# Mixing of the second block: four differential maps a step, a running bank for the suffix sums, paired value products, a new order; two weight differences on VectorE

## What is computed

```python
# per layer l = 0, 1 of the second block
f = swiglu(rmsnorm(x, ffn1_pre_g[l]), ffn1_w_gate[l], ffn1_w_up[l], ffn1_w_down[l])
x = x + FFN_RESIDUAL_WEIGHT * rmsnorm(f, ffn1_post_g[l])
m = token_mixing(rmsnorm(x, mix_pre_g[l]), w_in[l], rel_bias[l], ..., w_out[l], lambda_init)
x = x + rmsnorm(m, mix_post_g[l])
f = swiglu(rmsnorm(x, ffn2_pre_g[l]), ...)

def diff_attention(q, k, v, lam, subln_g, lambda_init):      # 4 heads, two maps of 32 features each
    ...
        sc = jnp.einsum('bqhmd,bkhmd->bhmqk', q[:, q0:kend], k[:, :kend]).astype(jnp.float32) * scale
        sc = sc + alibi[None, :, None]
        sc = jnp.where(allowed[None, None, None], sc, NEG_INF)
        p = jax.nn.softmax(sc, axis=-1)
        w = p[:, :, 0] - lam * p[:, :, 1]
        outs.append(jnp.einsum('bhqk,bkhd->bqhd', w.astype(v.dtype), v[:, :kend]))
    ...
def stick_breaking_attention(q, k, v):                       # 6 heads of 64
    ...
        z = jnp.einsum('bqhd,bkhd->bhqk', q[:, q0:kend], k[:, :kend]).astype(jnp.float32) * scale
        log_beta = jax.nn.log_sigmoid(z)
        log_one_minus = jnp.where(strict, jax.nn.log_sigmoid(-z), 0.0)
        suffix = lax.cumsum(log_one_minus, axis=3, reverse=True) - log_one_minus
        a = jnp.where(strict, jnp.exp(log_beta + suffix), 0.0)
        outs.append(jnp.einsum('bhqk,bkhd->bqhd', a.astype(v.dtype), v[:, :kend]))
```

## Time and profile before

| | |
|---|---|
| median of 3 runs | 2588.81 us (2588.8 to 2589.32) |
| the profiled execution | 2589.32 us, its span 2587.5 us |
| TensorE busy | 2560.7 us, 99% of the span |
| VectorE, ScalarE, GpSimd busy | 1637.7, 1169.8, 423.3 us |
| TensorE's granted clock | 1.000 in the mean |
| mixing of layer 0 and of layer 1 | 982 to 1246 us and 1969 to 2233 us |
| HBM | 97 GB/s over the span |

### The profile page before, as it was taken

How to read it: one execution, slowest core, us unless ns; L and a number is a source line. 1 busy time by engine, 2 the same in 40 slices (tenths; PEclk the granted TensorE clock), 3 DMA queues, 4 the chain that set the end, 5 groups by cost and what they waited for, 6 DMA issues and landing times.

```text
span 2587.5 us, 42242 instructions
## 1 busy us (share of the span) xinstructions
PE 2560.7 (99%) x17332; PEld 2222.2 (86%) x17332; DVE 1637.7 (63%) x2667; ACT 1169.8 (45%) x2019; POOL 423.3 (16%) x416
## 2 busy tenths in 40 slices
PE   9999999999999999999999999999999999999998
PEld 7788887678999888867899988999888876899987
DVE  3425653667999353456699735899444356699833
ACT  4123333643655234465455533555334456355522
POOL 0230010001332011111143200233001020133200
PEclk9999999999999999999999999999999999999999
DMA  8722140012333232211233332332323212223321
GB/s 323 290 93 93 38 123 33 34 58 82 99 106 107 98 117 67 66 50 66 82 115 100 113 114 66 115 115 98 114 82 104 64 50 83 66 90 115 115 96 67
DMA packets 183854, 252.73 MB, mean 98 GB/s; under 512 B 13040, under 2 KB 158448, under 8 KB 179184
## 3 DMA queue, kind: packets, MB, share of 16 engines
q1 hardware_dynamic: 183664, 250.04, 29.0%
HBM read 247.92 MB, written 2.10 MB: 97 GB/s over the span
## 4 chain that ended last, share of the span: by engine, by line
PE 92%; DVE 3%; ACT 2%; issue 1%; DMA 1%; POOL 1%; SPq 0%; POOLq 0%; ACTq 0%; DVEq 0%
PE psum L816 89%; PE psum L1384 1%; DMA mod_w<-in_l_ab_w_mod 1%; PE psum L1268 1%; PE psum L884 1%; DVE stats_first L2206 0%; DVE work L2199 0%; ACT w_hi L1558 0%; DVE X L2202 0%; ACT work L1606 0%; POOL stats_first L2925 0%; PE psum L860 0%; DVE h_lo L2138 0%; DVE wide L2236 0%; POOL stats L2980 0%
## 5 line engine op out<-in xcount | busy, mean ns | idle before, releaser
L816 PE MATMUL psum<-h_hi,w_hi 128*128 128x256 f32 (+1 forms) x1520 | 498.2, 328 | 0.4 <-DVE w_lo L2105 0.3
L816 PE MATMUL psum<-h_lo,w_hi 128*128 128x256 f32 (+1 forms) x1520 | 490.9, 323 | 0.0
L816 PE MATMUL psum<-h_hi,w_lo 128*128 128x256 f32 (+1 forms) x1520 | 490.8, 323 | 0.0
L2105 DVE TENSOR_TENSOR w_lo<-raw,w_hi 128x2048 fp32r<-128x2048 f32 (+1 forms) x99 | 223.4, 2260 | 295.1 <-ACT w_hi L1558 294.6
L816 PEld LDWEIGHTS psum<-h_hi,w_hi 128*128 128x128 f32 x1520 | 290.0, 191 | 32.6 <-issue 9.7
L816 PEld LDWEIGHTS psum<-h_hi,w_lo 128*128 128x128 f32 x1520 | 289.6, 191 | 22.6
L816 PEld LDWEIGHTS psum<-h_lo,w_hi 128*128 128x128 f32 x1520 | 289.9, 191 | 20.0 <-issue 0.5
L1558 ACT ACTIVATE w_hi<-raw 128x2048 fp32r<-128x2048 f32 (+1 forms) x100 | 188.5, 1888 | 259.5 <-PE psum L816 249.5
L816 PE MATMUL psum<-w_hi,ff_hi 128*128 128x512 f32 x576 | 225.2, 391 | 1.2 <-DVE ff_lo L2722 1.2
L816 PE MATMUL psum<-w_lo,ff_hi 128*128 128x512 f32 x576 | 224.4, 390 | 0.0
L816 PE MATMUL psum<-w_hi,ff_lo 128*128 128x512 f32 x576 | 224.4, 390 | 0.0
(11 more groups left out here) (364 smaller groups left out, 5444.4 us busy)
## 6 DMA issues: line engine op xcount, KB each, us to landing
raw<-in_ffn_w_gate SPq DMA_DIRECT2D x44, 1024.0 KB, 5.2
raw<-in_ffn_w_up SPq DMA_DIRECT2D x44, 1024.0 KB, 5.2
raw<-in_ffn_w_down SPq DMA_DIRECT2D x44, 1024.0 KB, 4.7
raw<-in_w_in SPq DMA_DIRECT2D x36, 512.0 KB, 5.0
raw<-in_l_ab_w_in SPq DMA_DIRECT2D x10, 1024.0 KB, 9.3
mod_w<-in_l_ab_w_mod SPq DMA_DIRECT2D x8, 1024.0 KB, 17.9
raw<-in_w_out SPq DMA_DIRECT2D x8, 1024.0 KB, 4.8
raw<-in_cd_w_in SPq DMA_DIRECT2D x7, 1024.0 KB, 5.3
```

The costliest lines, as they stand in the source:

```text
L816: return pe.matmul(o, lhsT, rhs, start=start, stop=stop, skip_group_check=True)
L2105: dve.tensor_tensor(lo[:, 0:nk * n], raw[c % 2][:, 0:nk * n], hi[:, 0:nk * n].bitcast(F32), ALU.subtract).then_inc(*w_lo_made.mark(key))
```

## The change

- *Scores:* a step `diff_quad` multiplies the two maps of two heads, four products on four row groups, into four banks. The soft ring gets four banks, the stick ring keeps two.
- *Suffix sums:* a head's four stages share one bank and go from the last stage to the first. Each stage after the first waits until VectorE has subtracted the one before, adds the product of `strict` with that stage's softplus (triangle plus strict mask is all ones), and then the product of `tri` with its own. VectorE subtracts in the same order, and the bank comes free at the end.
- *Value products:* those of two heads follow each other directly and write to two halves of 128 columns of one bank (bands and differential heads); VectorE or ScalarE reads the first when both are done.
- *Order:* all four strings are new.
- *Feed-forward:* S3 and S4 move from GpSimd to VectorE, after the split of A22.

```diff
@@ mix_streams
-    streams["a"] = [step for i in range(0, len(bands), 2) for step in [("band_pair", *streams["a"][i][1:]), *streams["a"][i:i + 2]]]
+    for letter, both in (("a", "band_pair"), ("c", "band_value_pair"), ("d", "diff_quad"), ("g", "diff_value_pair")):
+        single = streams[letter]
+        streams[letter] = [step for i in range(0, len(single), 2) for step in [(both, *single[i][1:]), *single[i:i + 2]]]
...
-                           [("stick_sums", h, kt) for kt in range(NT)] + [("stick_exp", h)] + [("stick_value_pair", h)] * (letter == "s") +
+                           [("stick_sums", h, kt) for kt in reversed(range(NT))] + [("stick_exp", h)] + [("stick_value_pair", h)] * (letter == "s") +
@@ MIX_ENGINES, MIX_LETTERS (TensorE's string of before, then of after; the others are rewritten in the same way)
...
-    "pe": ("vppspspsaapbpbppppappbbppppcpcappppppppppcbcppcppttbppssbpdtpptppdfppadpssppsppcpppbpspspsfbpccpppabppppcppdpbafbdpppppc"
-           "ssgttgttpffgdpcsspdpppcsdfspspspbbppgappppfdggfdppdfpfdgpgpppfcdggppfdgcstbfdbggastfdccttssfabbsccabbgnfgccbbpcpaogcppnp"
-           "pppppnbobppppppccooprpppnpppppppprppppr"),
+    "pe": ("ppppaasppbpsbpsapppbpcpppbppppppppppppppppbscaptbpspsptsdpptcpbpppbpftpfppdscpppspsaapsppbppbppppppsgcpbfppsppbaptstdp"
+           "pfstppgcbftpfpspdpbpasppsgcspppppfpdpfpppfgsfpdppptbsbactsbgbtcfsnftdgsafppobabpfpgcppdnppbbpopcappfppbbppofncgppnpprp"
+           "pppprovpppppppr"),
@@ tensor_program, mixing
-                proj, soft, stick = Ring([0, 1]), Ring([2, 3, 4]), Ring([5, 6, 7])
+                proj, soft, stick = Ring([0, 1]), Ring([2, 3, 4, 5]), Ring([6, 7])
...
+                    at = b * BANK + 64 * (h % 2)
...
-                    elif kind == "diff_scores":
+                    elif kind == "diff_quad":
                         _, i, h, t = step
                         width = (t + 1) * P
...
+                        banks = [claim(soft.take(), ("bs", s, i + n // 2, n % 2)) for n in range(4)]
+                        if t == 0:
+                            pe.wait_ge(*mix_kept[s, 1408 + P * (h // 2)])
+                        for n, b in enumerate(banks):
+                            p0 = 32 * n
+                            done(mm(bank(b, width), q_b[p0:p0 + 32, h // 2, t * P:(t + 1) * P], k_b[p0:p0 + 32, h // 2, 0:width], True, True),
+                                 ("bs", s, i + n // 2, n % 2))
...
-                    elif kind == "diff_values":
+                    elif kind == "diff_value_pair":
...
+                        bank_of["bv", s, i + 1] = b
...
+                        for odd in range(2):
+                            pe.wait_ge(*probs_turned["b", s, i + odd])
+                            done(attend(v_b, h + odd, t, b, turned["b"][(i + odd) % 2]), ("bv", s, i + odd))
...
-                        b = claim(stick.take(), ("csum", s, h, kt))
-                        if kt == 0:
+                        if kt == NT - 1:
+                            claim(stick.take(), ("csum", s, h))
                             pe.wait_ge(*stick_cut[s, h])
                             pe.wait_ge(*stick_landed[layer])
-                        m = mm(bank(b, L - kt * P), tri[:, :], soft_[:, STARTS[kt]:STARTS[kt] + L - kt * P], True, kt == 3)
-                        for k2 in range(kt + 1, NT):
-                            m = mm(bank(b, L - k2 * P, (k2 - kt) * P), ones[:, :], soft_[:, STARTS[k2]:STARTS[k2] + L - k2 * P], False, k2 == 3)
+                        else:
+                            pe.wait_ge(*stick_dve["sums", s, h, kt + 1])
+                            mm(full(("csum", s, h), L - (kt + 1) * P, (kt + 1) * P), strict[:, 0, :], soft_[:, STARTS[kt + 1]:STARTS[kt + 1] + L - (kt + 1) * P],
+                               False, False)
+                        m = mm(full(("csum", s, h), L - kt * P, kt * P), tri[:, :], soft_[:, STARTS[kt]:STARTS[kt] + L - kt * P], kt == NT - 1, kt == 0)
                         done(m, ("csum", s, h, kt))
@@ vector_program, ffn
+                def last_mixed(key):
+
+                    s2, s3, s4 = (fast_weights(key, name)[2] for name in ("S2", "S3", "S4"))
+                    dve.tensor_tensor(s3, fast_block(key, 0, 0), fast_block(key, 0, 1), ALU.subtract).then_inc(*fast_mixed.mark((key, "S3")))
+                    dve.wait_ge(*fast_first[key, "S2"])
+                    dve.tensor_tensor(s4, fast_block(key, 1, 0), s2, ALU.subtract).then_inc(*fast_mixed.mark((key, "S4")))
...
                         lo_blocks(following, "A1")
                         lo_blocks(following, "A22")
+                        last_mixed(following)
@@ gpsimd_program
-                    if s[0] == "ffn":
-                        for q, key in enumerate(fast_keys(s[1], layer)):
...
-                            pool.tensor_tensor(mixed_["S3"], fast_block(key, 0, 0), fast_block(key, 0, 1), ALU.subtract).then_inc(*fast_mixed.mark((key, "S3")))
-                            pool.wait_ge(*fast_first[key, "S2"])
-                            pool.tensor_tensor(mixed_["S4"], fast_block(key, 1, 0), mixed_["S2"], ALU.subtract).then_inc(*fast_mixed.mark((key, "S4")))
```

More of the change, by code:

```diff
@@ L245 @@
 BAND_ITEM = {(step[2], step[3]): step[1] for step in MIX_ORDER["dve"] if step[0] == "band_scores"}
-DIFF_ITEM = {(step[2], step[3]): step[1] for step in MIX_ORDER["pe"] if step[0] == "diff_scores"}
+DIFF_ITEM = {(step[2], step[3]): step[1] for step in MIX_ORDER["dve"] if step[0] == "diff_scores"}
 def build(nc, A, out):
@@ L1433, in mixing @@
                         turn_probs(("at", s, i), band_slot(i), t)
-                    elif kind == "band_values":
+                    elif kind == "band_value_pair":
                         _, i, h, t = step
                         b = claim(soft.take(), ("av", s, i))
+                        bank_of["av", s, i + 1] = b
                         if h in (0, 4):
                             pe.wait_ge(*mix_kept[s, "v", int(h == 4), t])
-                        pe.wait_ge(*probs_turned["a", s, i])
-                        done(attend(v_a, h, t, b, turned["a"][i % 2]), ("av", s, i))
-                    elif kind == "diff_scores":
+                        for odd in range(2):
+                            pe.wait_ge(*probs_turned["a", s, i + odd])
+                            done(attend(v_a, h + odd, t, b, turned["a"][(i + odd) % 2]), ("av", s, i + odd))
+                    elif kind == "diff_quad":
                         _, i, h, t = step
                         width = (t + 1) * P
[L1444 to L1449, removed]
+                        banks = [claim(soft.take(), ("bs", s, i + n // 2, n % 2)) for n in range(4)]
[5 more added lines that the diff above has]
+                                 ("bs", s, i + n // 2, n % 2))
                     elif kind == "diff_turn":
@@ L1453, in mixing @@
                         turn_probs(("bt", s, i), map0[i % 2], t)
-                    elif kind == "diff_values":
+                    elif kind == "diff_value_pair":
                         _, i, h, t = step
                         b = claim(soft.take(), ("bv", s, i))
+                        bank_of["bv", s, i + 1] = b
                         if h == 0:
                             pe.wait_ge(*mix_kept[s, "v", 3, t])
-                        pe.wait_ge(*probs_turned["b", s, i])
-                        done(attend(v_b, h, t, b, turned["b"][i % 2]), ("bv", s, i))
+                        for odd in range(2):
+                            pe.wait_ge(*probs_turned["b", s, i + odd])
+                            done(attend(v_b, h + odd, t, b, turned["b"][(i + odd) % 2]), ("bv", s, i + odd))
                     elif kind == "stick_part":
@@ L2037, in mixing @@
                         event = ("bv", s, i)
-                        copy(o_tok[:, t, 384 + h * 64:384 + (h + 1) * 64], event, full(event, 64), attn_kept, (s, i), scale=stat("diff", i, 6, 7))
+                        act.wait_ge(*psum_full["bv", s, i | 1])
+                        copy(o_tok[:, t, 384 + h * 64:384 + (h + 1) * 64], event, full(event, 64, 64 * (h % 2)), attn_kept, (s, i), scale=stat("diff", i, 6, 7))
+                        freed["bv", s, i - h % 2] = attn_kept[s, i]
                     elif kind == "stick_scores":
@@ L2056, in mixing @@
                         z = stick_ring[h % 2][1]
-                        act.wait_ge(*stick_dve["sums", s, h, 3])
+                        act.wait_ge(*stick_dve["sums", s, h, 0])
                         act.activation(z[:, :], z[:, :], ACT.Exp).then_inc(*stick_step.mark(("weights", s, h)))
@@ L2734, in ffn @@
                     lo_blocks(keys[0], name)
+                last_mixed(keys[0])
                 for name in ("S1", "S2"):
@@ L2870, in mixing @@
                         event, width, o = ("csum", s, h, kt), L - kt * P, STARTS[kt]
-                        if kt == 0:
+                        if kt == NT - 1:
                             dve.wait_ge(*stick_cut[s, h])
```

(6 more changed lines are left out.)

29 lines of the change are left out of this document (11 added, 18 removed).

## The result

The changed kernel takes 2562.19 us in the median of four runs (2560.91 to 2564.18); the kernel before, beside it on the same chip, 2589.07 (2588.8 to 2589.8). The ratio is 0.9896, with a 95% interval of 0.9879 to 0.9914: 26.9 us less, 1.0%. The forecast was 2553.5, so the time lies inside the range and 8.7 us above the forecast; taken by itself, it is the 2562 of rival 1 and of the lower end of rival 2. Those 8.7 us are what the experiments look for. The profiled execution took 2564.18 us.

The account below looks back on a forecast made before the run. The prediction took TensorE's own queue to bound the kernel. Its terms, -10.4 - 8.6 - 16.9 + 1 = -34.9 us from 2588.8, gave 2553.9, stated as 2553.5 us, with a range of 2543 to 2567.

Parts of the forecast that it names:

- rival 1: Four-map steps don't overlap fourfold, or the switch price belongs partly to semaphore waits that stay: 2562 us, chance 0.10.
- rival 2: VectorE's emptying of banks holds TensorE in the mixing's last third, 4 to 8 us a layer more: 2562 to 2570, chance 0.12.
- TensorE bounds the kernel: Whole kernel: only time taken out of TensorE's own queue, or a new wait put into it, can move the end.
- Suffix sums: Mixing: 512 columns of products with ones gone from each of twelve heads, -10.4 us, all in TensorE's queue.
- Four maps at once: Mixing scores: eight steps of four maps replace 16 of two, all four side by side, -4.3 us a layer, -8.6 in all.
- Fewer switches: TensorE's order in the mixing: 47 fewer tiling changes a layer, 94 in all, at 0.18 us each, -16.9 us.
- S3 and S4 at 0: Feed-forward: moving the two subtractions to VectorE costs 1.36 us a key, 1.37 comes back with GpSimd idle: 0 us.
- Rival 3: VectorE becomes the bound of the feed-forward parts, needing 11.0 us for a key of 10.1: 2618 us, chance 0.04.
- The gain row: Loading and scaling the next gain row moves to just ahead of token tile 2: +0.5 us a layer, +1, bounds 0 and +6.
- Rival 4: The chain of suffix sums stalls at each stage on VectorE's subtraction, 36 waits: about 2589 us, chance 0.03.
- Rival 5: The mixing's waits of 5 us a layer vanish: 2544 us, chance 0.06.
- The waits in the new order: Mixing: TensorE's unexplained waits stay at 5 us a layer, bounds 0 and 10, so -10 to +10 in all.

Follow-up runs that it names:

- c_after: The changed kernel itself run again, beside three of the follow-up kernels on one chip: 2563.85 us, ratio 0.9903.
- e7: e1 with the value products of stick-breaking heads 4 and 5 put ahead of those of differential items 10 and 11 in TensorE's order: 2550.19 us.
- e1: The changed kernel with GpSimd masking the last stage first and each stage waiting only for its own masks, not all eight of a head: 2548.88 us.
- e2: The changed kernel with twelve extra 128-column products ahead of the wait for the masks at heads 0 and 2, the wait kept: 2558.72 us.
- e5: The changed kernel with an extra full-array 128-column product between the two value products of each pair, 40 in all: 2588.15 us.
- e6: The changed kernel with an extra 128-column product, as two column halves side by side, between the value products of each pair: 2572.96 us.

## Why the prediction was right, and where it missed

*TensorE bounds the kernel; only its own queue counts:* right. 24.8 of the 25.1 us are in the mixings, and 10 us of VectorE's time saved in the feed-forward window moved nothing.

*Suffix sums, -10.4:* right; undone alone it costs 9.8 to 11.5.

*Four maps at once, -8.6:* right. The timeline of the changed kernel at full width:

```profile
1122.12 1.14 PE L818 MATMUL psum<-k_b,q_b 32*128 32x512 f32 x8
1123.19 0.50 PE L818 MATMUL psum<-h_hi,w_hi 128*128 128x512 f32 x1
```

Eight records take 1.07 us from start to start, 0.86 of columns and 0.2 more, against 1.06 for four records in the earlier trace rows. The narrower ones take 0.86, 0.64 and 0.43, again 0.2 more than their columns. Rival 1 (1.9 us) is out. The estimate of 1.12 that I had worked out from the Trainium skill (TensorE: Matmul & The Clock Gate, "Packing small matmuls") was 0.05 too high here.

*Fewer switches, -16.9:* right in mechanism and nearly in size. The price measured by itself is 0.18 at full clock, in two kernels whose waits at those places are the same, so the second half of rival 1 is out too; the account by kinds of change gives 7.9 us a layer where 47 x 0.18 = 8.5, since the places that went are on average a little cheaper. With the columns that is 34.7 us instead of 35.9.

*S3 and S4 at 0:* right, and more came back than I summed: VectorE is at 161.37 us of 180, not 171. I had counted two groups of instructions that get faster, 1.37 us a key. Others were slowed by GpSimd too, such as the sum of 768 columns (L2716, now L2735: 1401 ns before, 959 after). Rival 3 is out.

*The gain row, +1:* about right. In the profiled run no such wait stands; in c_after there is one of 0.80 us (1214.51, released by VectorE's scaled tile) in layer 0, in e7 one of 1.36 in layer 1 (2174.75). It comes and goes between executions, and may be part of why the medians of one kernel differ by 1.7 us; that was not tested.

*Rival 2, VectorE holds TensorE in the last third:* seen once a layer, and small:

```profile
1166.81 0.93 PE L818 MATMUL psum<-k_b,q_b 32*128 32x384 f32 x8
1168.48 0.45 PE L818 MATMUL psum<-v_b,work 128*64 128x64 f32 x8 [0.75 <-DVE stats_mix L2857]
```

The stalls of before, such as the one of the earlier trace rows, are gone in turn. *Rival 4, a stall at each stage of a sum,* isn't seen in the waits. *Rival 5, waits that vanish,* came partly true in e1, where 3.0 us a layer are left instead of 5.7.

*The waits in the new order, 5 us a layer as before:* **this is the step that failed.** They went from 5.7 to 10.9. The sum with the measured terms is 2589.3 - 34.7 + 10.4 = 2565.0 for the profiled execution, which took 2564.2. So this term alone comes out at +10.4, just past its own bound of +10. That the time still lies in the range is in part luck: the range was wider by half of rival 2, whose cause is not the one at work. I had looked for danger where the windows showed VectorE nearly full, in the last third, and had treated the new order as a whole. Two things were there to be read and weren't. The step of the sum waits for all eight masks of a head, and the new letters put the masks of head 0 next to it: from the first mask to head 0's first sum it was 26.5 us, and became 3.8, where the masks need 3.4 even when nothing holds them up. And in costing S3 and S4 I had used the very behaviour that makes this too short: that a GpSimd instruction and a VectorE one with two SBUF inputs hold each other up. There it was VectorE that got its time back; in the mixing it is GpSimd that is held up, five masks a layer, and TensorE's queue stands behind them. The Trainium skill (SBUF — State Buffer, "Who interferes with whom") states this in both directions, whichever issues first; by that rule the trace agrees, with 1.80 and 2.50 us beside VectorE's 1.49 and 2.59.

The second half of the miss is a price that was not in the sum at all: the earlier trace rows showed a clock of 1.00 everywhere, and I wrote that it had nothing to give. It had something to take. Each pause of 2.3 to 2.9 us cost another 1.7 at half clock, so by these windows such a wait costs 1.6 to 1.7 times its length; by the medians it is less, since e1 gave back 13.3 us for waits of 10.5.

That the masks, and through them the clock, are the cause is shown by e1 and e2. That the masks would have been in time without VectorE's two instructions is worked out from their rows, with 0.4 us to spare at head 0; no kernel with those two instructions moved was run. A kernel with the running bank in the order of before was not run either, so what the new order alone is worth is open.

With the masks per stage the kernel takes 2548.9 us, 1.55% less than before and 4.6 below the forecast: the change was worth more than I had said, and gave a third of that back at two waits a layer.

## What to carry to other kernels

When an order is rewritten, go through every wait of the engine that bounds the kernel and write down how long before it its releaser's work starts; a semaphore that stands for eight small instructions should be split as soon as the consumer needs only the first two, and the instructions put in the order in which they are needed. Count GpSimd's instructions at their held-up length wherever VectorE runs long two-input instructions beside them, and count a pause of TensorE of some 2 to 3 us with the half clock that follows it. And group products of one tiling: at 0.18 us for each change, an ordering that saves 94 changes (15.8 us by the account) is worth more here than removing 512 columns from each of 12 heads.

## What the runs showed of the hardware

- After TensorE was idle for 2.91 us (and for 2.34), its granted clock was 0.50 for part of the next 5 us, 1.7 us lost each time. With products in the pause it stayed 1.00. In the 0.25 us pauses of e1 it stayed 1.00 too.
- GpSimd's 128x128 instruction of 0.46 us took 1.64 to 2.51 us when a VectorE instruction with two SBUF inputs ran beside it; VectorE's 128x512 split took 1.79 instead of 0.68 when GpSimd ran beside it. The hold-up goes both ways.
- A change between full-array and half-array tiling costs 0.18 us of TensorE's time at full clock (35 places of e5 against e6), and 0.19 in the mean of all 80 changes, five places with half clock among them.
- Four fp32 products on 32 rows each, in four banks, run fully side by side: 1.07 us at 512 columns, against 1.06 for two of them.
- A long idle time may have "issue" as its releaser even where a semaphore of another engine ends it; with work in front of the wait, the same place named GpSimd.
